# A two-layer decoder step on one core: gate logits with the weights stationary, an unsplit fp32 gather, last sums spread by 64-row tiles

## The chip, the cores and the metric

The kernel runs on one core of a Trainium2 chip. The time is device microseconds of that core; the time before is 1553.24 us, the median of three runs (1552.7 to 1557.6). In the profile, PE is TensorE's matmuls and PEld its weight loads, DVE is VectorE, ACT ScalarE, POOL GpSimd, SP SyncE, which issues nearly all loads. An fp32 matmul leaves two records in the trace; one whose operands are both of type fp32r leaves one.

## The reference, cut to what matters

One step of a two-layer model over T = 264 tokens (256 of a prompt, 8 of samples), D = 1024. Layer a has a gated DeltaNet mixer with 8 heads and a dense SwiGLU, layer b a pooling mixer and a top-2-of-8 mixture of experts; both attend to memory. The change touches three places of it.

```python
# layer_a: two logits for each head come from one projection
proj = u @ w_in
qkv, z, b_logit, a_logit, cq = jnp.split(proj, [o1, o2, o3, o4], axis=-1)
beta = jax.nn.sigmoid(b_logit)
g = -jnp.exp(a_log) * jax.nn.softplus(a_logit + dt_bias)
...
# layer_b: h + moe_swiglu(rmsnorm(h, norm2), ...)
logits = (x @ router_w).astype(jnp.float32)
top_v, top_i = lax.top_k(logits, TOP_K)
gates = jax.nn.softmax(top_v, axis=-1)
for e in range(N_EXPERTS):
    y = y + dispatch[..., e:e + 1] * swiglu(x, wi[e], wo[e])
...
y_prompt = rmsnorm(hp, final_norm)
```

## The kernel before

TensorE multiplies dense weights as split products: each 128x2048 tile of a weight comes by DMA into one of two draw slots, ACT copies its high part to fp32r (dense_high, L363), DVE subtracts to get the low part (dense_low, L369), and TensorE makes three fp32r products a pair (L1757). The tiles run in the order of the list DENSE. The draw slot is free once the low part exists; SP then issues the next load.

**Gate logits.** Before the input projection of layer a, 24 matmuls (L1821) take the normalised tokens u as the stationary operand, 128 tokens at a time, and the 16 columns of wba as the moving one; the token rows of logits land in bank 1. ACT copies them into gba (L661, L662) and runs exponent and logarithm for the gates; behind these in its queue stand the convolution history (L677), the evictions of the first projection tiles (L720) and the high part of the next weight. TensorE goes on with a_tile(0) and the rest (a_tile(t), 24 products each), once DVE has evicted the last memory values (mem_kv, L1029).

**Gather.** After the last b_out tile the router's logits are ranked on DVE; sel (rt_sub) goes to TensorE, which counts positions in each expert's list (bank 6). DVE makes a 0/1 matrix disp for each of three token tiles (L1589) and the normalised token rows xtok (token_rows, L1576). ACT and DVE split xtok into xth and xtl (L935, L1597); TensorE runs four unread matmuls on a ring chunk (L2290), then 48 passes of 96 columns that gather the first expert's tokens, feature-major, high into PP[3], low into PP[2] (L2297); ACT copies the one and DVE adds the other (L940, L1611). That is xs_ready for the first expert step.

**Experts.** A step serves 96 slots of one expert (C = SG x SL = 3 x 32). up(c) for 32 chunks makes 3 x 4 matmuls of 448 columns each, slots stationary, four at a time in column strips of 32 (L2316); down(j) for 14 chunks makes 12 of 512 columns (L2326) into banks 6 and 7, where slots 64 to 95 lie in bank 7 (z2) as two halves of the sum. The weights stream through a ring of 14.7 MB: 16 up chunks or 14 down chunks. SP issues a load as soon as TensorE has used the chunk that lay there (w_used; load_up L462, load_down L466). The rows of each step go to DRAM (slot_rows) by POOL's queue, and the next step's rows come from there and are turned in blocks of 32x32 by DVE (L1709). The number of steps is read from nsteps_i; eight run here.

**Last sums.** In the last step TensorE turns the matrix chosen (last_rows, L2351); POOL fetches each token's rows of the earlier steps (L590), DVE adds them (L1669). The last step's own rows go by matmul: rows_out puts the pieces of banks 6 and 7 together in yslot (L1675 to L1680), ACT and DVE split them (L959, L1717), TensorE spreads them to tokens by 12 matmuls (L2373), and DVE adds, normalises and hands on (last_part L1729, final L1735; ACT squares in L969).

Of the kernel before, what the change touches and what calls it, by code (L numbers as in the profile page):

```python
# [26 lines left out]
P = 128  # L27
D = 1024
# [41 lines left out]
LOADS = [3] * RDOWN + [2] * (RUP - RDOWN)  # L70
EARLIER = [2, 2, 2, 2, 3, 3, 2] + [0] * 9
# [42 lines left out]
def build(nc, ins, outs):  # L114
    ctx = ExitStack()
    with ctx:
# [9 lines left out]
        wba = sb("wba", KD * 16)  # L126
# [74 lines left out]
        assert 22336 + 2 * 12 * T == WREG  # L201
        cq = cut(gen, 0, XH * T).rearrange("p (m c) -> p m c", m=XH)
# [70 lines left out]
        disp = gat_("disp", 13312, 3 * C, F32R)  # L273
        xth = gat_("xth", 3072, 3 * D, F32R)
        xtl = gat_("xtl", 6656, 3 * D, F32R)
# [50 lines left out]
        picked, posb = cut(small, 760, 32), cut(small, 792, 32)  # L326

# [52 lines left out]

        def by_quarters(t, n):
            return xtok[0:n, t, :].rearrange("p (q k i) -> p k q i", q=4, k=KD)

        def turned_view(x, t, n):
            return x[0:n, t * D:(t + 1) * D].rearrange("p (k q i) -> p k q i", q=4, k=KD)

        def gathered(out):
            return out[:, :].rearrange("p (k n) -> p k n", n=P)[:, :, 0:C].rearrange("p k (s c) -> p s k c", s=SG)
# [134 lines left out]
        def _(pool):  # L523
# [38 lines left out]
            for x in (xth, xtl):  # L562
                pool.memset(x[:, 2 * D:3 * D].bitcast(F32), 0.0).then_inc(s("rest_zero"), 1)
# [32 lines left out]
        def _(a):  # L596
# [66 lines left out]
            a.wait_ge(s("gba_out"), 2)  # L663
# [250 lines left out]
            for t in range(KD - DSET):  # L914
                next_high(AT["b_out", t])
                if t == 4:
                    a.wait_ge(s("xt_mm"), 4)
                    a.wait_ge(s("zeroed"), 5)
                    token_square(2, 0, slice(0, 512))
                    a.activation(home[2][0:NS, 0:512], bank(5)[0:NS, :], ACT.Copy).then_inc(s("xt_out"), 1)  # L920
# [1550 lines left out]
```

## Time and profile before

| | us |
|---|---|
| median of three runs | 1553.24 |
| the profiled execution | 1551.51 |
| its span, first to last instruction | 1549.9 |
| PE busy | 1517.6 (98%) |
| DVE busy | 568.1 (37%) |
| ACT busy | 358.3 (23%) |
| mean granted TensorE clock | 0.990 of 2.4 GHz |
| chain: share of L2316 + L2326 | 37% + 19% |
| chain: share of L1757 | 24% |

The numbers are of one execution. A line of the chain gives the start, the length, the engine, the tile written, the line and how many records. In a timeline a bracket at the end is the time for which the engine was idle before, and what ended that. In the table by stretches, busy time for each of the five rows of engines is followed by the count of instructions, then come the granted clock as a share of full speed, the share of the DMA engines that is busy, and GB/s. A busy TensorE is not one at its peak: ends of matmuls are modelled.

### The profile page before, as it was taken

To read this page: it belongs to the slowest core of one execution; us is meant where nothing else is said; L and a number is where in the kernel's file an instruction comes from. 1 tells how busy PE (TensorE), PEld (TensorE's weight loads), DVE (VectorE), ACT (ScalarE), POOL (GpSimd) and SP (SyncE) were. 2 spreads that over 40 slices of the span, in tenths; PEclk is the share of its full clock that TensorE was granted. 3 is DMA by queue.
4 is the path that set the end of the run, shared out by engine and by line. 5 is a ranking of instruction groups with operands and counts; after the bars stand their busy time and mean duration, and the time that the engine had idled before them with its cause. 6 is when DMAs were issued, how large, how long until landed. Compare 5 with 4: busy or idle time off the path is not lost.

```text
span 1549.9 us, 32644 instructions
## 1 busy us (share of the span) xinstructions
PE 1517.6 (98%) x14378; PEld 883.2 (57%) x14378; DVE 568.1 (37%) x948; ACT 358.3 (23%) x587; POOL 60.4 (4%) x101
## 2 busy tenths in 40 slices
PE   8999999899999999999999999999999999999996
PEld 8989888899999999833233233232332332332332
DVE  6767878666665577510111101101101101111114
ACT  6466544444443453410000000000000000000001
POOL 0000031000000000020000000000000000000010
PEclk9999999999999999999999999999999999999998
DMA  7764358254554575799999999999999999999993
GB/s 266 286 234 175 110 190 261 72 204 170 185 190 150 196 301 198 277 404 416 419 401 419 419 400 420 418 400 420 401 419 419 400 419 419 400 420 418 419 416 122
DMA packets 78053, 490.97 MB, mean 317 GB/s; under 512 B 9305, under 2 KB 9561, under 8 KB 53217
## 3 DMA queue, kind: packets, MB, share of 16 engines
q1 hardware_dynamic: 70000, 460.71, 74.7%
q0 software_dynamic: 7920, 28.25, 5.6%
q8 instruction: 113, 1.85, 0.5%
q14 instruction: 20, 0.16, 0.0%
HBM read 465.00 MB, written 23.92 MB: 315 GB/s over the span
## 4 chain that ended last, share of the span: by engine, by line
PE 89%; DVE 5%; ACT 3%; DMA 2%; issue 1%; SPq 0%; DVEq 0%; ACTq 0%
PE PP L2316 37%; PE PP L1757 24%; PE PP L2326 19%; PE PP L2062 1%; PE PP L2072 1%; DVE dlo L369 1%; ACT dhi L363 1%; DMA ring<-in_mkv 1%; PE PP L1869 0%; PE PP L1853 0%; PE PP L2202 0%; PE PP L1845 0%; PE PP L2050 0%; PE PP L1831 0%; DMA ring<-in_a_out 0%
## 5 line engine op out<-in xcount | busy, mean ns | idle before, releaser
L2316 PE MATMUL PP<-ring,gen 128*32 128x448 f32 x6144 | 581.2, 541 | 1.0 <-DVE gen L1611 1.0
L2316 PEld LDWEIGHTS PP<-ring,gen 128*32 128x32 f32 x6144 | 185.0, 110 | 396.1 <-issue 394.9
L2326 PE MATMUL PP<-ring,gen 128*32 128x512 f32 x2688 | 289.8, 592 | 0.0
L1694 DVE TENSOR_TENSOR gen<-ubuf,PP 128x448 f32<-128x448 f32 x48 | 26.9, 616 | 519.1 <-PE PP L2316 519.1
L1757 PE MATMUL PP<-uh,dhi 128*128 128x264 f32 x736 | 214.4, 291 | 1.8 <-DVE dlo L369 1.1
L369 DVE TENSOR_TENSOR dlo<-ring,dhi 128x2048 fp32r<-128x2048 f32 (+2 forms) x85 | 175.5, 2064 | 98.0 <-ACT dhi L363 97.7
L1757 PE MATMUL PP<-ul,dhi 128*128 128x264 f32 x736 | 210.1, 285 | 0.0
L1757 PE MATMUL PP<-uh,dlo 128*128 128x264 f32 x736 | 209.8, 285 | 0.0
L952 ACT ACTIVATE ubuf<-PP 128x448 f32<-128x448 f32 x48 | 22.6, 545 | 782.6 <-PE PP L2316 782.6
L2326 PEld LDWEIGHTS PP<-ring,gen 128*32 128x32 f32 x2688 | 81.5, 110 | 205.7 <-issue 205.7
L363 ACT ACTIVATE dhi<-ring 128x2048 fp32r<-128x2048 f32 (+2 forms) x85 | 147.1, 1730 | 106.0 <-PE PP L1757 80.6
L1757 PEld LDWEIGHTS PP<-uh,dhi 128*128 128x128 f32 x736 | 140.0, 190 | 7.6 <-issue 5.4
L1757 PEld LDWEIGHTS PP<-ul,dhi 128*128 128x128 f32 x736 | 140.0, 190 | 0.2
L1757 PEld LDWEIGHTS PP<-uh,dlo 128*128 128x128 f32 x736 | 139.4, 189 | 0.0
L1675 DVE COPY gen<-PP 32x512 f32<-32x512 f32 x16 | 11.0, 686 | 231.7 <-PE PP L2326 231.5
L1757 PE MATMUL PP<-cath,dhi 128*128 128x264 f32 x192 | 56.3, 293 | 1.8 <-DVE dlo L369 1.8
L1757 PE MATMUL PP<-cath,dlo 128*128 128x264 f32 x192 | 55.2, 287 | 0.0
L1757 PE MATMUL PP<-catl,dhi 128*128 128x264 f32 x192 | 55.2, 287 | 0.0
L1757 PE MATMUL PP<-hidh,dhi 128*128 128x264 f32 x176 | 50.3, 286 | 0.6 <-DVE dlo L369 0.6
L1757 PE MATMUL PP<-hidh,dlo 128*128 128x264 f32 x176 | 50.0, 284 | 0.0
L1757 PE MATMUL PP<-hidl,dhi 128*128 128x264 f32 x176 | 49.8, 283 | 0.0
L1757 PEld LDWEIGHTS PP<-cath,dhi 128*128 128x128 f32 x192 | 36.7, 191 | 3.1 <-DVE dlo L369 2.4
(457 smaller groups left out, 1387.5 us busy)
## 6 DMA issues: line engine op xcount, KB each, us to landing
ring<-in_w_up SPq DMA_DIRECT2D x256, 896.0 KB, 22.6
ring<-in_w_down SPq DMA_DIRECT2D x112, 1024.0 KB, 23.1
ring<-in_wi SPq DMA_DIRECT2D x22, 1024.0 KB, 4.8
ring<-in_a_in SPq DMA_DIRECT2D x18, 1024.0 KB, 5.2
ring<-in_wo SPq DMA_DIRECT2D x16, 704.0 KB, 4.0
slot_rows<-ring POOLq DMA_DIRECT2D x25, 384.0 KB, 16.0
ring<-in_mkv SPq DMA_DIRECT2D x8, 1024.0 KB, 5.1
ring<-in_kc SPq DMA_DIRECT2D x8, 1024.0 KB, 9.3
```

The lines of the kernel that those rows point to most:

```text
L363: a.activation(halves(n)[0], x, ACT.Copy).then_inc(s("d_hi"), 1)
L369: v.tensor_tensor(low, draw[n % DRAW][:, 0:WIDTH[DENSE[n][0]]], high.bitcast(F32), ALU.subtract)\
L952: a.activation(esil[g], bank(g)[:, 0:FQ], ACT.Silu).then_inc(s("up_sil"), 1)
L1675: v.tensor_copy(yslot[2 * SL:C, 512 * h:512 * (h + 1)], z2[64 * h:64 * h + SL, :]).then_inc(s("y_part"), 1)
L1694: v.tensor_tensor(hslot[g], esil[g], bank(SG + g)[:, 0:FQ], ALU.mult).then_inc(s("up_h"), 1)
L1757: mm = pe.matmul(out, lhs[l], rhs[r], start=first and i == 0, stop=last and i == 2)
L2062: mm = pe.matmul(PP[c][:, head(x)], MLb[c][:, head(x)], Tb[c][:, head(x)], start=True, stop=True)
L2072: mm = pe.matmul(PP[c][:, head(x)], Xb[c][:, head(x)], Ub[c][:, head(x)], start=True, stop=True)
L2316: mm = pe.matmul(bank((c // KD % 2) * SG + g)[SL * q:SL * (q + 1), 0:FQ], xs[:, at_:at_ + SL], w[:, q * FQ:(q + 1) * FQ], start=(k == 0), ...
L2326: return pe.matmul(out[SL * quarter:SL * (quarter + 1), :], hT[:, at_:at_ + SL], w[:, k * D + h * 512:k * D + (h + 1) * 512], start=(j == ...
```

## The change

Three edits in one kernel. (1) Gate logits: wba is padded to 32 columns for each k and becomes the stationary operand, u the moving one; the eight k go to four strips of 32 columns, two each. ACT copies the 128x264 result, and after a_tile(0) three small matmuls with sel16 (a 0/1 matrix that DVE sums from ident) add the four strips and turn them to token rows (gate_columns). wba moves into the area of cq. (2) Gather: xtok and disp stay fp32 and unsplit; disp is stationary in groups of 32 slots, xtok moves in four quarters of 256 columns side by side; the result lies slot-major in banks 4, 6 and 7, and DVE turns it by block transposes straight from PSUM into xs. Of the four unread matmuls two go ahead of the wait for rt_sub. POOL zeroes xtok's third tile. (3) Last sums: banks 7 and 6 are copied whole, by DVE as soon as the last z2 product is done and by ACT at the end, and are spread as they stand: chosen holds each slot's row where it lies in those banks, TensorE turns six 128x128 tiles of it, and multiplies 64 rows by 32 columns at a time. Semaphore counts follow; sd_cols and sd_blk are merged.

```diff
+GATHER_BANK = [4, 6, 7]
...
+        wba = cut(gen, 0, KD * 32)
...
-        disp = gat_("disp", 13312, 3 * C, F32R)
-        xth = gat_("xth", 3072, 3 * D, F32R)
-        xtl = gat_("xtl", 6656, 3 * D, F32R)
+        disp = cut(gen, 13312, 3 * C)
...
-        yth, ytl = gat_("yth", 3072, D, F32R), gat_("ytl", 6656, D, F32R)
...
-        spread = gat_("spread", 8704, 384, F32R)
-        chosen = cut(gen, 9088, 3 * C)
+        spread = cut(gen, 8000, 3 * 2 * P)
+        yz = [cut(yslot, 0, 512), cut(yslot, 512, 512)]
+        chosen = cut(gen, 9088, 3 * 2 * P)
...
+        sel16 = cut(small, 824, 16)
...
-            for x in (xth, xtl):
-                pool.memset(x[:, 2 * D:3 * D].bitcast(F32), 0.0).then_inc(s("rest_zero"), 1)
+            pool.memset(xtok[:, 2, :], 0.0).then_inc(s("rest_zero"), 1)
...
             a.wait_ge(s("logits_mm"), 1)
+            a.activation(rt[:, 0:T], bank(1)[:, 0:T], ACT.Copy).then_inc(s("gba_out"), 1)
+            a.wait_ge(s("logits_mm"), 2)
...
-            a.wait_ge(s("rest_zero"), 2)
-            for t in range(3):
-                n = P if t < 2 else NS
+            for t in range(2):
                 a.wait_ge(s("xt_tok"), t + 1)
-                a.activation(turned_view(xth, t, n), by_quarters(t, n), ACT.Copy).then_inc(s("xt_hi"), 1)
-            for t in range(2):
                 a.activation(home[t], PP[t][:, :], ACT.Copy).then_inc(s("xt_out"), 1)
 
-            a.wait_ge(s("gat_mm"), 1)
-            a.activation(xs.rearrange("p (s k c) -> p s k c", s=SG, k=KD), gathered(PP[3]), ACT.Copy).then_inc(s("xt_out"), 1)
...
                     a.wait_ge(s("pos_mm"), 2)
-                    a.activation(spread[0:C, :], bank(0)[0:C, 0:384], ACT.Copy).then_inc(s("xt_hi"), 1)
+                    a.activation(spread, PP[0][:, 0:3 * 2 * P], ACT.Copy).then_inc(s("xt_hi"), 1)
                     a.activation(yroot[:, 0:1], epsc[:, 0:1], ACT.Sqrt)
-                    for g in range(2):
-                        a.wait_ge(s("y_part"), st * 2 + (g + 3))
-                        a.activation(yth[0:C, g * 512:(g + 1) * 512], yslot[0:C, g * 512:(g + 1) * 512], ACT.Copy)\
-                            .then_inc(s("xt_hi"), 1)
+                    a.wait_ge(s("w_used"), st * PERX + PERX)
+                    a.wait_ge(s("y_stored"), st * 16 + 16)
+                    a.activation(yz[0], bank(6), ACT.Copy).then_inc(s("xt_hi"), 1)
...
+            v.reduce_sum(sel16, ident.rearrange("p (g c) -> p c g", g=4)[:, 0:16, :], AX).then_inc(s("zeroed"), 1)
...
+            v.wait_ge(s("rest_zero"), 1)
             token_rows(2)
-            v.wait_ge(s("rest_zero"), 2)
-            for t in range(3):
-                n = P if t < 2 else NS
-                v.wait_ge(s("xt_hi"), t + 1)
-                v.tensor_tensor(turned_view(xtl, t, n), by_quarters(t, n), turned_view(xth, t, n).bitcast(F32), ALU.subtract).then_inc(s("xt_lo"), 1)
...
-            v.wait_ge(s("gat_mm"), 2)
-            v.wait_ge(s("xt_out"), 5)
-            xs4 = xs.rearrange("p (s k c) -> p s k c", s=SG, k=KD)
-            v.tensor_tensor(xs4, xs4, gathered(PP[2]), ALU.add).then_inc(s("xs_ready"), 1)
+            v.wait_ge(s("gat_mm"), 1)
+            for g in range(SG):
+                ins_ = v.transpose(xs[:, g * 2 * P:(g + 1) * 2 * P], bank(GATHER_BANK[g])[:, 0:2 * P])
+            ins_.then_inc(s("xs_ready"), 1)
...
-                    v.tensor_scalar(chosen[:, t * C:(t + 1) * C], iota[:, 0:C], row_late[:, t:t + 1], None, ALU.is_equal)\
-                        .then_inc(s("disp"), 1)
+                    for at_, n, slots in ((0, 2, iota[:, 0:2 * SL]), (P, 4, iota[:, 2 * SL:C])):
+                        v.tensor_scalar(chosen[:, 2 * t * P + at_:2 * t * P + at_ + P].rearrange("p (n c) -> p n c", n=n),
+                                        slots.unsqueeze(1).to_broadcast([P, n, P // n]), row_late[:, t:t + 1], None, ALU.is_equal)\
+                            .then_inc(s("disp"), 1)
...
-                v.wait_ge(s("w_used"), st * PERX + PERX)
                 v.wait_ge(s("y_stored"), st * 16 + 16)
-                rows_out(st, last)
                 if last:
-                    for g in range(2):
-                        v.wait_ge(s("xt_hi"), g + 5)
-                        v.tensor_tensor(ytl[0:C, g * 512:(g + 1) * 512], yslot[0:C, g * 512:(g + 1) * 512],
-                                        yth[0:C, g * 512:(g + 1) * 512].bitcast(F32), ALU.subtract).then_inc(s("xt_lo"), 1)
+                    v.wait_ge(s("z2_done"), 1)
+                    v.tensor_copy(yz[1], bank(7)).then_inc(s("xt_lo"), 1)
+                else:
+                    v.wait_ge(s("w_used"), st * PERX + PERX)
+                    rows_out(st)
...
-            for t in range(3):
-                n = P if t < 2 else NS
-                for k in range(KD):
-                    mm = pe.matmul(bank(1)[0:n, 16 * t:16 * t + 16], u[:, k, t * P:t * P + n], wb[:, k, :],
-                                   start=(k == 0), stop=(k == KD - 1))
+            for k in range(KD):
+                j = k % 4
+                mm = pe.matmul(bank(1)[32 * j:32 * j + 32, 0:T], wb[:, k, :], u[:, k, :], start=(k < 4), stop=(k >= 4))
             mm.then_inc(s("logits_mm"), 1)
+
+            def gate_columns():
+                pe.wait_ge(s("gba_out"), 1)
+                pe.wait_ge(s("zeroed"), 2)
+                for t in range(3):
+                    n = P if t < 2 else NS
+                    mm = pe.matmul(bank(1)[0:n, 16 * t:16 * t + 16], rt[:, t * P:t * P + n], sel16, start=True, stop=True)
+                mm.then_inc(s("logits_mm"), 1)
...
-            for t in range(5):
+            a_tile(0)
+            gate_columns()
+            for t in range(1, 5):
...
+            pe.wait_ge(chunk_loaded[0], 16 * EARLIER[0] + 16)
+
+            def unread(count):
+                for _ in range(count):
+                    pe.matmul(bank(7), up_of(0)[:, 0:P], up_of(0)[:, 0:512], start=True, stop=True)
+
+            unread(2)
...
-            pe.wait_ge(s("xt_out"), 2)
-            pe.wait_ge(chunk_loaded[0], 16 * EARLIER[0] + 16)
-            for _ in range(4):
-                pe.matmul(bank(5), up_of(0)[:, 0:P], up_of(0)[:, 0:512], start=True, stop=True)
-            pe.wait_ge(s("disp"), 3)
-            pe.wait_ge(s("rest_zero"), 2)
-            for x, done, out in ((xth, "xt_hi", PP[3]), (xtl, "xt_lo", PP[2])):
-                pe.wait_ge(s(done), 3)
-                for k in range(KD):
-                    for t in range(3):
-                        mm = pe.matmul(out[:, k * P:k * P + C], x[:, t * D + k * P:t * D + (k + 1) * P], disp[:, t * C:(t + 1) * C], start=(t == 0), stop=(t == 2))
-                mm.then_inc(s("gat_mm"), 1)
+            unread(2)
+            pe.wait_ge(s("rest_zero"), 1)
+            for t in range(3):
+                pe.wait_ge(s("disp"), t + 1)
+                pe.wait_ge(s("xt_tok"), t + 1)
+                for g in range(SG):
+                    for q in range(4):
+                        mm = pe.matmul(bank(GATHER_BANK[g])[SL * q:SL * (q + 1), 0:2 * P], disp[:, t * C + g * SL:t * C + (g + 1) * SL],
+                                       xtok[:, t, 2 * P * q:2 * P * (q + 1)], start=(t == 0), stop=(t == 2))
+            mm.then_inc(s("gat_mm"), 1)
             pe.wait_ge(s("xt_out"), 4)
-            pe.wait_ge(s("xt_tok"), 2)
...
-                def down(j):
+                def down(j, apart=False):
                     landed(st, j, 2)
                     w = down_of(j)
 
@@ -2329,7 +2321,9 @@
 
                     for h in range(2):
                         for k in range(2):
-                            product(z2, 2 * h + k, 2, k, h)
+                            mm = product(z2, 2 * h + k, 2, k, h)
+                    if apart:
+                        mm.then_inc(s("z2_done"), 1)
...
-                    pe.wait_ge(s("disp"), 6)
-                    pe.wait_ge(s("up_sil"), st * (2 * SG) + (SG + 1))
-                    for t in range(3):
-                        mm = pe.transpose(bank(0)[0:C, t * P:(t + 1) * P], chosen[:, t * C:(t + 1) * C], ident)
+                    pe.wait_ge(s("disp"), 9)
+                    pe.wait_ge(s("up_sil"), st * (2 * SG) + (SG + 2))
+                    for t in range(6):
+                        mm = pe.transpose(PP[0][:, t * P:(t + 1) * P], chosen[:, t * P:(t + 1) * P], ident)
                     mm.then_inc(s("pos_mm"), 1)
                 pe.wait_ge(s("y_out"), st + 1)
                 for j in range(NDOWN):
                     if j in (0, NDOWN // 2):
                         pe.wait_ge(s("h_turned"), st * 2 + (1 if j == 0 else 2))
-                    down(j)
+                    down(j, last and j == NDOWN - 1)
...
-            pe.wait_ge(s("xt_hi"), 4)
+            pe.wait_ge(s("xt_hi"), 1)
             for t in range(3):
-                n = P if t < 2 else NS
-                for g in range(2):
-                    for x, done, had in ((yth, "xt_hi", 5), (ytl, "xt_lo", 4)):
-                        if t == 0:
-                            pe.wait_ge(s(done), g + had)
-                        mm = pe.matmul(PP[t][0:n, g * 512:(g + 1) * 512], spread[0:C, t * P:t * P + n], x[0:C, g * 512:(g + 1) * 512],
-                                       start=(done == "xt_hi"), stop=(done == "xt_lo"))
+                n = SL if t < 2 else NS
+                for z, done, count in ((1, "xt_lo", 1), (0, "xt_hi", 2)):
+                    if t == 0:
+                        pe.wait_ge(s(done), count)
+                    for x in range(2):
+                        rows_ = slice(64 * x, 64 * x + 64)
+                        for q in range(4 if t < 2 else 1):
+                            at_ = (2 * t + z) * P + SL * q
+                            mm = pe.matmul(bank(2 * t + x)[SL * q:SL * q + n, :], spread[rows_, at_:at_ + n], yz[z][rows_, :],
+                                           start=(z == 1), stop=(z == 0))
```

## Rows read from the trace of the kernel before

**Rows 1.** The page: GB/s moved by the DMA, in 40 equal slices of the span.
```profile
GB/s 266 286 234 175 110 190 261 72 204 170 185 190 150 196 301 198 277 404 416 419 401 419 419 400 420 418 400 420 401 419 419 400 419 419 400 420 418 419 416 122
```

**Rows 2.** The chain that ended last: start us, us, engine, tile, line, count.
```profile
60.88 4.12 PE PP L1821 x48
...
362.77 116.30 PE PP L1757 x960
...
663.23 74.83 PE PP L2316 x768
...
774.12 72.16 PE PP L2316 x768
...
1496.00 36.23 PE PP L2326 x336
```

**Rows 3.** Line L466 (down loads): one issue each near 731 and 1486 us, and landing.
```profile
L466 SPq DMA_DIRECT2D ring<-in_w_down x1: 333/333/333, 731.5 to 731.5; - x1
...
DMA to landing us min/median/max: 16.2/16.2/16.2
...
L466 SPq DMA_DIRECT2D ring<-in_w_down x1: 328/328/328, 1486.6 to 1486.6; - x1
...
DMA to landing us min/median/max: 31.1/31.1/31.1
```

**Rows 4.** Busy time by engine, then granted clock (PEclk), DMA share, GB/s, by stretch.
```profile
65.00:66.00 1.00, 1.00 (x5) 1.00 (x6) 0.57 (x3) 0.95 (x3) 0.00 (x0) 0.50 1.08 328
...
652.00:654.00 2.00, 2.00 (x4) 0.88 (x3) 1.97 (x6) 0.75 (x2) 0.00 (x0) 0.50 1.02 427
```

**Rows 5.** The chain again: matmuls in column strips (L1853, L1896) and row strips (L2036).
```profile
90.23 1.86 PE PP L1853 x32
...
122.33 0.48 PE PP L1896 x8
...
239.27 1.14 PE PP L2036 x8
```

**Rows 6.** Timelines of DVE, then of ACT, 60 to 80 us: start, us, what, [idle before].
```profile
61.07 0.87 DVE L1029 TENSOR_SCALAR gen<-PP,gen 128x256 f32<-128x256 f32 x2
...
74.53 2.29 DVE L369 TENSOR_TENSOR dlo<-ring,dhi 128x2048 fp32r<-128x2048 f32 x1 [4.93 <-ACT dhi L363]
...
65.03 0.20 ACT L661 ACTIVATE small<-PP 128x32 f32<-128x32 f32 x1 [2.15 <-PE PP L1821]
...
72.50 1.91 ACT L363 ACTIVATE dhi<-ring 128x2048 fp32r<-128x2048 f32 x1
...
78.05 0.39 ACT L720 ACTIVATE gen<-PP 128x264 f32<-128x264 f32 x1 [2.53 <-PE PP L1757]
```

**Rows 7.** The chain from 650 to 664 us: the third token row tile, then the gather.
```profile
653.86 1.27 DVE gen L1576
...
656.35 5.84 PE PP L2297 x48
...
662.22 0.96 DVE gen L1611
```

**Rows 8.** Timelines of 640 to 670 us, and of DVE from 735 us.
```profile
647.57 0.60 ACT L911 ACTIVATE ubuf<-PP 128x512 f32<-128x512 f32 x1 [8.61 <-PE PP L2224]
...
650.59 5.38 PE L2290 MATMUL PP<-ring 128*128 128x512 f32 x8
...
741.54 1.05 DVE L1709 STREAM_TRANSPOSE gen<-gen 128x256 f32<-128x256 f32 x3
```

**Rows 9.** Timeline of the last 18 us, DVE's rows.
```profile
1532.35 1.40 DVE L1675 COPY gen<-PP 32x512 f32<-32x512 f32 x2 [9.62 <-PE PP L2326]
...
1539.05 1.28 DVE L1729 SCALAR_TENSOR_TENSOR gen<-PP,gen 128x1024 f32<-128x1024 f32 x1 [1.08 <-PE PP L2373]
...
1540.76 1.28 DVE L1729 SCALAR_TENSOR_TENSOR gen<-PP,gen 128x1024 f32<-128x1024 f32 x1 [0.42 <-PE PP L2373]
...
1546.34 1.27 DVE L1735 SCALAR_TENSOR_TENSOR gen<-gen 8x1024 f32<-8x1024 f32 x1
```

More of the change, by code:

```diff
@@ L125, in build @@
         gains = sb("gains", GN)
-        wba = sb("wba", KD * 16)
         router = sb("router", KD * E)
@@ L379, in cache_of @@
             return cut(ring, ARENA + x * 2048, 2048)
[L381 to L388, printed above, removed]
         def new_state(v, r):
@@ L662, in _ @@
             a.activation(gba[0:NS, 2, :], bank(1)[0:NS, 32:48], ACT.Copy).then_inc(s("gba_out"), 1)
-            a.wait_ge(s("gba_out"), 2)
+            a.wait_ge(s("gba_out"), 3)
             a.activation(gb, gba[:, :, 0:8], ACT.Exp, scale=-1.0).then_inc(s("gate_exp"), 1)
@@ L917, in _ @@
                     a.wait_ge(s("xt_mm"), 4)
-                    a.wait_ge(s("zeroed"), 5)
+                    a.wait_ge(s("zeroed"), 6)
                     token_square(2, 0, slice(0, 512))
@@ L1086, in _ @@
             next_low(7)
-            v.wait_ge(s("gba_out"), 2)
+            v.wait_ge(s("gba_out"), 3)
             dt_b = gains[:, GDT:GDT + H].unsqueeze(1).to_broadcast([P, 3, H])
@@ L1111, in _ @@
             v.wait_ge(s("conv_rows"), NS)
-            v.wait_ge(s("zeroed"), 2)
+            v.wait_ge(s("zeroed"), 3)
             def prompt_max(l, t):
@@ L1180, in _ @@
                     l2_scale(4, 8)
-            v.wait_ge(s("logits_mm"), 2)
+            v.wait_ge(s("logits_mm"), 3)
             link(v.tensor_copy(cG, bank(5)[:, 0:16]))
@@ L1229, in sample_columns @@
                 v.tensor_copy(padded(kpad), by_group(kq[:, :, 0]))
-                v.tensor_tensor(kqd, kq[:, :, 0], kq[:, :, 1], ALU.mult).then_inc(s("sd_cols"), 1)
+                v.tensor_tensor(kqd, kq[:, :, 0], kq[:, :, 1], ALU.mult).then_inc(s("sd_in"), 1)
             def level_mask(lv, c):
@@ L1321, in block @@
                 v.tensor_tensor(ublk[r % 2].rearrange("p (n c) -> p n c", c=P), urow.unsqueeze(1).to_broadcast([P, 4, P]),
-                                own16[:, 4 * r:4 * r + 4].unsqueeze(2).to_broadcast([P, 4, P]), ALU.mult).then_inc(s("sd_blk"), 1)
+                                own16[:, 4 * r:4 * r + 4].unsqueeze(2).to_broadcast([P, 4, P]), ALU.mult).then_inc(s("sd_in"), 1)
             for lv in range(1, NLVL):
@@ L1461, in _ @@
             ins_.then_inc(s("zeroed"), 1)
-            v.wait_ge(s("zeroed"), 4)
+            v.wait_ge(s("zeroed"), 5)
             def pooled(n):
@@ L1554, in _ @@
                     v.memset(yslot, 0.0).then_inc(s("y_out"), 1)
-            v.wait_ge(s("logits_mm"), 3)
+            v.wait_ge(s("logits_mm"), 4)
             link(v.tensor_copy(rout, bank(4)[:, 0:3 * E]))
@@ L1670, in collect, with rows_out @@
                                        in1=(home, y1)[j][t][0:n, :], op0=ALU.mult, op1=ALU.add).then_inc(s("y_sum"), 1)
-            def rows_out(st, last):
+            def rows_out(st):
                 z1, z2 = bank(6), bank(7)
@@ L1680, in rows_out @@
                     ins_ = v.tensor_tensor(half, half, z2[64 * h + SL:64 * (h + 1), :], ALU.add)
-                    if last:
-                        ins_.then_inc(s("y_part"), 1)
-                    elif h:
+                    if h:
                         ins_.then_inc(s("y_out"), 1)
@@ L1828, in scores @@
                 if l == 0 and t == 0:
-                    pe.wait_ge(s("gba_out"), 2)
+                    pe.wait_ge(s("gba_out"), 3)
                 for x in range(XH):
@@ L2017, in _ @@
             pe.wait_ge(s("dl_mt"), 4)
-            pe.wait_ge(s("sd_cols"), 1)
+            pe.wait_ge(s("sd_in"), 1)
             pe.wait_ge(s("state_loaded"), 64)
@@ L2029, in outer @@
             def outer(r):
-                pe.wait_ge(s("sd_blk"), r + 1)
+                pe.wait_ge(s("sd_in"), r + 2)
                 if r == 0:
@@ L2427 @@
         "grow2": rows(f["b_norm2"]),
-        "wba": w_in[:, split:split + 16].reshape(KD, P, 16).transpose(1, 0, 2).reshape(P, -1),
+        "wba": np.pad(w_in[:, split:split + 16].reshape(KD, P, 16), ((0, 0), (0, 0), (0, 16))).transpose(1, 0, 2).reshape(P, -1),
         "router": f["b_router"][0].reshape(KD, P, E).transpose(1, 0, 2).reshape(P, -1),
```

1 line of the change is left out of this document (removed).

## The prediction

> **What bounds the kernel now.** I read the page's slices first, then the chain that ended last, then the landing times of the expert weights, and at last the timelines and the granted clock around the three places that the change touches. In the slices the reader is to see two halves: up to about 660 us the DMA comes and goes, from there on it moves about 419 GB/s in nearly every slice but the last [rows 1]. The chain gives that second half to TensorE: each of eight expert steps is 72.16 us of up products (74.83 in the first) and some 36.2 of down products, with nothing between [rows 2]. So TensorE is the bound by the chain. The landing times say how near DMA is to being it too. The twelfth down load of the first step (index 11) was issued at 731.5 and landed 16.2 later, at 747.7 [rows 3]; TensorE needed it at 663.23 + 74.83 + 11 x 2.588 = 766.5 (36.23 / 14 = 2.588 a down tile) [rows 2], a lead of 18.8 us. The tenth (index 9) of the last step was issued at 1486.6 and landed 31.1 later, at 1517.7 [rows 3]; its use is at 1496.00 + 9 x 2.588 = 1519.3 [rows 2]. The lead has melted to 1.6 us. A load is issued when its ring slot comes free, and the time to land has grown from 16 to 31 us: the queue always holds work, and delivers a little more slowly than TensorE eats. This reading decides most here.
>
> **Part 1, gate logits.** Now 24 matmuls with u stationary, 16 columns each, take 4.12 us (L1821) [rows 2], and TensorE comes out of them at its 1.2 GHz level: 0.50 is granted from 65 to 66 us [rows 4]. The change runs 8 matmuls of 264 columns, their weights 32 columns wide, in four column strips: two groups of four. Four strips with 288 columns took 0.48 [rows 5], so two groups of 264 take 0.88. ACT copies the sums out while it has nothing else to do, and three small matmuls after a_tile(0) turn them to token rows: six records at 4.12 / 48 = 0.09, 0.5 us. A tile of the input projection is 24 records, 116.30 / 40 = 2.91 [rows 2]. New order on TensorE: logits until 61.8; a_tile(0) must wait for DVE's last memory value, made at 61.94 [rows 6], and the added reduce_sum stands ahead of it in DVE's queue for some 0.2, so 62.1; gates end at 62.1 + 2.9 + 0.5 = 65.5; three more tiles end at 74.3, where ACT saw the fourth tile end at 78.05 before [rows 6]. For TensorE that is 3.7 us. Late next is ACT's queue: the gate copies and their chain (two table loads, eight history copies) stand ahead of the evictions and of the next high half. The gate copy ran at 65.03 and will run at about 65.6, so the chain behind it moves back by 0.6. The high half of a_in 2 started at 72.50, because it stood behind an eviction that waited for TensorE; now it starts at about 71.0, right behind the gates and two evictions that find their tiles done, and the low half ends 4.3 us later (72.50 to 74.53 + 2.29 now) at 75.3 [rows 6]. TensorE waits 1 us there. Net **-2.8 us**. Bounds: -4.4 (all of 4.12 and about 1.2 of slow start, less 0.88, if ACT holds nothing back) and -1.5 (only what the high half moves by). From there to 645 us the chain runs from TensorE through ACT and DVE back to TensorE, all of it released by TensorE, so the shift is carried on; the expert loads wait for the last b_out tile and start as much sooner.
>
> **Part 2, the gather.** Removed: high halves on ACT (L935), low halves on DVE (L1597), 48 passes of 96 columns (5.84 us, L2297), ACT's copy (L940), DVE's addition (0.96, L1611) [rows 7]. Added: 36 matmuls of 256 columns in four strips, three groups per token tile, and three block transposes from PSUM. DVE's chain sets the order: the third token row tile runs from 653.86 to 655.13 [rows 7]. The four unread matmuls ran from 650.59 for 5.38 us [rows 8], mostly at the low level (0.50 granted from 652 to 654 [rows 4]), after an idle stretch in which TensorE waited for rt_sub. Two of them now run in that stretch. At 2.4 GHz one takes 0.86 (512 columns, by 72.16 / 96 = 0.75 for four strips of 448 side by side [rows 2], which stream as long as one), so two are done when rt_sub comes, the other two by 652.5, and the clock has less reason to fall. With DVE as it is until 655.13, the last token tile's three groups start at 655.2. A group costs 1.86 / 4 = 0.465 by L1853 [rows 5], or 256/448 of 0.75 = 0.43 by the up products [rows 2]: 1.35 in all, until 656.6. Three transposes took 1.05 from SBUF (L1709) [rows 8]; from PSUM between that and 1.3, at 656.6 + 1.2 = 657.8 experts start, not at 663.23: -5.4. With a high clock the first up phase also loses its slow start, 74.83 - 72.16 = 2.67 [rows 2]. The move offers **8.0 us**; with the clock as low as before (groups and unread matmuls twice as long) about 2. ACT's copies of the residual (home) and the step count come earlier too, as their queues lose the halves, and hold nobody.
>
> **How much of the 8.0 is kept.** A faster start does not empty the DMA queue, which holds 16 to 31 us of work throughout. The loads' start does not move with the gather, so their landings don't. A TensorE that starts 8 us sooner only runs into them: the lead falls from 18.8 by some 2.4 us a step now; from 10.8 it is gone before the last steps, and these wait for weights. The down products end no sooner than 1517.7 + 5 x 2.588 = 1530.6 [rows 3] against 1496.00 + 36.23 = 1532.23 [rows 2]. Kept: **-1.6 us**. Six 128x128 transposes in place of three 128x96 ones (some 0.5 us more in the last step) vanish in the same wait, as do the six wider DVE writes in last_rows. Ends of this term: 0 (in another execution the landings come that much later) and -7.5 (they come earlier, and only the transposes cost).
>
> **Part 3, the last sums.** Now DVE puts four pieces together from 1532.35 on, ACT and DVE split them, TensorE multiplies 12 times, DVE adds tile 0 at 1539.05 and tile 1 at 1540.76, and its last instruction starts at 1546.34 [rows 9]. After: bank 7 is complete a third into the last down tile, so DVE's copy of it hides under the rest; ACT copies bank 6 (0.60, as its square of 128x512 from PSUM [rows 8]) while TensorE multiplies the other half. Then eight matmuls of 64 rows x 32 columns x 512 per half and tile. No row shows this shape. Four row strips of 32 at 512 columns took 1.14 (L2036) [rows 5], four column strips would take 0.86. If both directions combine, eight cost 0.9 to 1.1; if one does, 1.7 to 2.1; if none does, 6.9. I take 1.0, since each kind is seen to overlap. From the end of the down products (1532.23 in the old times) tile 0 is ready at 1534.3, tile 1 at 1536.3. Behind tile 1 DVE and ACT run as now: 1540.76 - 1536.3, **-4.4 us**. At 2.0 per eight, tile 1 comes at 1540.3 and the gain is 0.5.
>
> The Trainium skill has a rule that speaks against the strips of all three parts: TensorEngine Tiling (Array Packing), section Key Properties, says that a change of tiling mode drains the engine. The page gives no price; by it the sum would rise by one drain for each of some eight added changes. The trace shows no such gap where the last step goes from strips to whole-array transposes and back.
>
> **The sum.** -2.8 - 1.6 - 4.4 = -8.8 us. The profiled execution took 1551.51 (span 1549.9 and 1.6 around it), so 1542.7. The median of the runs shown, 1553.24, is 1.7 above it; I carry that over: **1544.5**.
>
> **The rivals.** (a) The landings have room that the issue rule hides, and the gather keeps 7.5: -2.8 - 7.5 - 4.4 = -14.7, 1538.5. For it: TensorE has no wait for a weight in this profile. Against: the time to land doubles over the steps. The Trainium skill's page DMA: Bandwidth & Descriptors, section Where 436 GB/s comes from, puts the ceiling at 435 GB/s; at that rate weights would come in time, which gives (a), but the slices hold about 419. (b) Strips of 64 rows and of 32 columns don't combine: -2.8 - 1.6 - 0.5 = -4.9, 1548.3. (c) Most is eaten: ACT's queue leaves -1.5 of part 1, the landings are no earlier than the old need, and the last sums run at 1.2 GHz: -2.5, 1550.7. For it: a lead of 1.6 us is smaller than the 4.9 between the three runs. (d) Slower: 64-row matmuls overlap with nothing. Place: the last sums; tile 1 comes at 4 x 6.9 = 27.6 behind the down products, not at 8.5: +19.1 - 4.4 = +14.7, 1568. It decides from 3.2 us per eight, where 4 x 3.2 = 8.5 + 4.4. Against it: each kind of strip overlaps.
>
> **Chances.** Forecast 0.54, (a) 0.13, (b) 0.18, (c) 0.11, (d) 0.04. The range goes from (a) past (b): 1538.5 to 1549, and leaves out (c) and (d). About 0.3% (4.7 us) is what a measurement of this kernel can tell from no change, so 1548.6 parts faster from same: the forecast, (a) and two thirds of (b) lie below, 0.79; the rest of (b) and (c) are same, 0.17; (d) is slower, 0.04.
>
> **What would show it.** Gates: tile 4 of a_in starts 2.8 us sooner, after about 1 us of waiting for DVE's low half. Gather: the first up product comes 5.4 us sooner behind the last b_out tile, at 2.4 GHz. Experts: the first steps last 108.4 us, the last ones more, with TensorE waiting for ring<-in_w_up and in_w_down; if no such wait appears, (a) holds. Last sums: about 1 us per eight matmuls, and 13.3 us from the last down product to the end of the span in place of 17.7. A time above 1549 would mean that strips don't combine or the leads were gone already.

## The result, and the profile after

The changed kernel takes 1544.44 us (median, 1543.83 to 1547.69) where the kernel before takes 1554.99 in the same comparison: ratio 0.9933, 95% interval 0.9922 to 0.9944. The forecast was 1544.5. The profiled execution took 1544.28; its span, first to last instruction, is 1542.5, 7.4 us less than before.

The slices of the page (GB/s, in 40 slices of the span), to compare with [rows 1]. The second half moves what it moved before:

```profile
GB/s 265 294 243 165 110 191 263 82 194 167 190 181 162 182 301 197 273 398 418 419 399 420 419 402 419 412 408 420 403 418 420 401 419 419 402 419 419 418 416 186
```

Part 1 in the chain of waits, 61 to 79 us (start, length, engine, tile, line, records), to compare with [rows 2, 6]:

```profile
61.32 0.80 DVE gen L1014 x2
...
62.16 3.20 PE PP L1738 x24
65.36 0.50 PE PP L1809 x6
...
71.19 1.81 ACT dhi L363
...
73.12 2.30 DVE dlo L369
75.42 0.04 issue
75.47 3.19 PE PP L1738 x24
```

The gates and their turning (L1809) are over at 65.86, and a_in tile 4 starts at 75.47 behind DVE's low half, as the prediction had it (75.3). In the kernel before, that tile's first matmul starts at 77.85 and the next work behind it at 80.78; here these are 75.47 and 78.50. So at 80 us the shift is 2.3 us, not 2.8.

Part 2 in the same view, to compare with [rows 7, 8]:

```profile
646.68 1.80 PE PP L2271 x4
...
649.77 1.80 PE PP L2271 x4
651.57 1.44 PE PP L2289 x24
653.00 0.10 issue
653.10 2.83 PE PP L2289 x48
655.93 0.02 issue
655.95 1.12 DVE gen L1592 x3
657.08 0.04 issue
657.12 12.22 PE PP L2308 x125
```

L2271 are the unread matmuls, L2289 the gather (36 matmuls of two records, 4.27 us), L1592 the block transposes. Experts start 12.7 us behind the end of the last b_out tile (640.01 + 4.39 = 644.40), before 17.8. The granted clock is 1.00 from 640 to 672 us, where [rows 4] had 0.50.

The end of the experts and the last sums, to compare with [rows 2, 9], first in the chain and then DVE's first addition in the timeline:

```profile
1480.84 33.12 DMA ring<-in_w_down
1513.96 0.04 issue
1514.01 15.66 PE PP L2318 x144
1529.66 3.69 PE PP L2370 x64
1533.35 0.02 issue
1533.38 1.28 DVE gen L1710
...
1538.96 1.27 DVE gen L1716
```

```profile
1531.66 1.28 DVE L1710 SCALAR_TENSOR_TENSOR gen<-PP,gen 128x1024 f32<-128x1024 f32 x1 [2.88 <-PE PP L2370]
```

And the waits of TensorE's weight loads (PEld) for landings between 652 and 1535 us (total, times, longest), of which the kernel before had none:

```profile
PEld PP L2308 <- DMA ring<-in_w_up: 8.9, 24, 1.4
PEld PP L2318 <- DMA ring<-in_w_down: 5.6, 10, 1.3
```

Landings now hold up the end of the expert phase: what releases the last 144 records of down products (L2318) is a load that was under way for 33.12 us, queue included. TensorE itself did not stand still that long: its longest wait is 1.4 us, and the totals of 8.9 and 5.6 us are idle time of its weight loads, part of which lies under running matmuls. From the start of the last b_out tile to the end of the down products it is 889.65 us, before 891.23. From there to the end of the span, last sums included (L2370), it is 12.84, before 17.67. So the span's 7.4 us are 1.0 up to the last b_out tile (its start moves from 641.00 to 640.01), 1.6 in the gather and the experts, 4.8 at the end.

### The profile page after: what moved, and what is told of

It reads as the page before. It is cut to its first block, busy times and chain, and to the rows that moved or that the text cites. A ratio compares the mean times of both kernels' runs of the same rounds, so it can differ in the third digit from the quotient of the medians.

```text
span 1542.5 us, 32756 instructions
## 1 busy us (share of the span) xinstructions
PE 1511.4 (98%) x14439; PEld 1013.8 (66%) x14439; DVE 561.0 (36%) x944; ACT 354.5 (23%) x583; POOL 59.5 (4%) x100
## 4 chain that ended last, share of the span: by engine, by line
PE 79%; DMA 6%; DVE 6%; SPq 4%; ACT 3%; issue 1%; DVEq 0%; ACTq 0%
PE PP L2308 33%; PE PP L1738 22%; PE PP L2318 15%; DMA ring<-in_w_down 2%; SPq L453 2%; DVE dlo L369 2%; SPq L457 2%; DMA ring<-in_w_up 2%; ACT dhi L363 2%; PE PP L2051 1%; PE PP L2061 1%; DMA ring<-in_mkv 1%; PE PP L1856 1%; PE PP L1840 0%; PE PP L2191 0%
## 5 line engine op out<-in xcount | busy, mean ns | idle before, releaser
L2308 PEld LDWEIGHTS PP<-ring,gen 128*32 128x32 f32 x6144 | 294.6, 110 | 287.1 <-issue 259.9
L2318 PE MATMUL PP<-ring,gen 128*32 128x512 f32 x2688 | 293.2, 592 | 1.8 <-DMA ring<-in_w_down 1.8
L2318 PEld LDWEIGHTS PP<-ring,gen 128*32 128x32 f32 x2688 | 112.2, 110 | 179.0 <-issue 159.9
```

The source lines that it names most:

```text
L2308: mm = pe.matmul(bank((c // KD % 2) * SG + g)[SL * q:SL * (q + 1), 0:FQ], xs[:, at_:at_ + SL], w[:, q * FQ:(q + 1) * FQ], start=(k == 0), ...
L2318: return pe.matmul(out[SL * quarter:SL * (quarter + 1), :], hT[:, at_:at_ + SL], w[:, k * D + h * 512:k * D + (h + 1) * 512], start=(j == ...
```

## The experiments

**Each part alone.** The kernel before with the hunks of one of the three edits, and semaphore counts to match (in the last sums alone, for instance, `(1, "xt_lo", 4), (0, "xt_hi", 5)`, as the old gather has counted before). 

> The kernel before with part 1 alone (gate logits with weights stationary, turned after tile 0). Theory: the shift of 2.3 us at 80 us is partly given back between 320 and 361 us, where weight landings stand in the chain of waits, so about 1.0 us is left at the end of the last b_out tile and at the end: ratio 0.9993, 0.9990 to 0.9998. Rival (everything behind is released by TensorE, the shift arrives whole): -2.3 to -2.8 us, ratio 0.9982 to 0.9985. The last b_out tile ends at 644.1 by the theory, at 642.4 by the rival (645.1 before).

> The kernel before with part 2 alone (gather from unsplit fp32 tiles, four unread matmuls in two places). Theory: experts start about 5.1 us earlier and the first one runs 2.7 us faster at the full clock, but from then on weight landings bind: downs end 1.6 us earlier (1530.6 against 1532.2), ratio 0.9990 (0.9986 to 0.9994). Rival (the 1.6 us left in the changed kernel are an interaction with the other two parts, alone it gives the 8.0 us): ratio 0.9949. TensorE waits for in_w_up and in_w_down are near 0 by the rival, 10 us or more by the theory.

> The kernel before with part 3 alone (last sums from both banks copied whole, in 64-row tiles). Theory: it stands behind everything and nothing gives it back: from the end of the last downs to the end of the span 12.8 us instead of 17.7, -4.8 us, ratio 0.9969 (0.9965 to 0.9973). Rival (part of the 4.8 us comes with the landing-bound end of the downs in the changed kernel): -3 us or less, ratio 0.998. The three parts alone should add up to -7.4 us, the gain of the whole.

Measured: ratios 0.9992 (0.9982 to 1.0002), 0.9995 (0.9986 to 1.0004) and 0.9973 (0.9964 to 0.9982). Of the three only the last is clear of no change; for the others the traces must tell. Part 3 alone: 13.17 us from the down products to the end, -4.5. Part 2 alone: experts start 5.1 us sooner behind the last b_out tile, TensorE's weight loads then wait 27.6 us for in_w_up and 11.4 for in_w_down, and 0.5 us is left (890.71 against 891.23); the rival's 8.0 is out. Part 1 alone: the last b_out tile starts at 640.27, 0.7 us sooner. That is nearer to the theory's 1.0 than to 2.3, but one pair of traces doesn't settle it (this start varies by 1.4 us between traces with the same gates, see below), and the interval of the time reaches both. Whether the parts add up was to be seen beside the whole, on another chip:

> The changed kernel once more, timed beside the next three on one chip. Theory (the parts add up): the parts alone gave ratios 0.9992, 0.9995 and 0.9973, product 0.9960, so 0.9945 to 0.9960 here. Rival (the parts help each other): 0.9933 as in the first comparison or lower.

Measured 0.9941 (0.9928 to 0.9953), 1545.65 against 1554.9, between the theory's range and the rival. Each part alone is uncertain by 0.0009 or 0.0010, their product 0.9960 by some 0.0016, so the intervals meet and neither reading is excluded; the pauses told of below may be a reason why the ratio of the whole differs from chip to chip.

**A later start of the experts.**

```
-            unread(2)
+            unread(6)
             pe.wait_ge(s("rest_zero"), 1)
```

> The changed kernel with six unread matmuls in place of the second two, ahead of the gather: its start moves by four times 0.90 us = 3.6 us. Theory (weight landings bind the experts): the end does not move, 1544.4 us, at most +0.5; TensorE's waits for in_w_up and in_w_down shrink by about 3.6 us. Rival (TensorE binds, the gather's gain went elsewhere): +3.6 us, 1548.0 us.

Measured 1544.91 us (1544.07 to 1547.67), ratio 0.9956 (0.9944 to 0.9968). The changed kernel wasn't timed on this chip, so the times don't decide: its medians elsewhere are 1544.44 and 1545.65, but its ratios 0.9933 and 0.9941 would make the late start 2 to 4 us slower, and the kernel before alone has medians from 1551.8 to 1555.0 on the chips used here. The traces do decide. Experts start at 660.08, 3.1 us later behind the last b_out tile than in the changed kernel, and the down products end 890.80 us behind that tile's start. The two profiles of the changed kernel have 889.65 and 890.08, both with a pause of TensorE told of below; the half in_wi kernel at the end of this section, which from 365 us on is the changed kernel but for which token goes to which expert, and has no such pause in the first steps, has 890.07. So of 3.1 us later, 0.7 (against the last) to 1.15 arrive, more than the theory's 0.5 and far less than the rival's all. The waits of TensorE's weight loads:

```profile
PEld PP L2318 <- DMA ring<-in_w_down: 7.0, 13, 1.9
PEld PP L2308 <- DMA ring<-in_w_up: 5.4, 13, 1.0
```

They shrank by 2.1 us. Most of a shift of the start is lost, in either direction: landings bind.

**Earlier loads.**

```
-            for c in range(RUP):
+            for c in [0, 1, 2, 3, 15, 9, 8, 10, 11, 4, 5, 6, 7, 12, 13, 14]:
...
+                if c == 15:
+                    sp.wait_ge(s("outputs_stored"), 32)
+                if c in (9, 8):
+                    sp.wait_ge(s("d_lo"), TURN[AT["b_out", 6 if c == 9 else 7]] + 1)
+                if c == 10:
+                    sp.wait_ge(s("bout_mm"), KD - 1)
                 if c == 4:
                     sp.wait_ge(s("bout_mm"), KD)
-                    sp.wait_ge(s("outputs_stored"), 32)
                     sp.wait_ge(s("rows_zeroed"), 16 * (NST + 1))
                 load_up(0, c)
```

> The changed kernel with SyncE's first 16 expert loads in another order: after chunks 0 to 3 come chunk 15 (its place in the ring is free once the pool states are stored), 9 and 8 (free once the low parts of the last two b_out tiles are taken), 10 and 11 (free after the seventh b_out tile), then 4 to 7 and 12 to 14 after the eighth as now. The DMA queue then works through the 5 us around 640 in which it now stands still. Theory: TensorE becomes the bound again, downs end at 1523.3 to 1524.8 instead of 1529.7, time 1538.0 to 1539.6 (-4.9 to -6.4 us against the changed kernel, ratio 0.989 to 0.990 to the kernel before). Rival: no change, 1544.4 us.

> Early loads as above and six unread matmuls as above, together. Theory: now TensorE is the bound, so the later start of 3.6 us that costs nothing in the changed kernel costs nearly all of itself: +2.2 to +3.6 us against the early loads alone, about 1541.6 us. Rival: the same time as early loads alone.

> The kernel before with SyncE's early loads alone. Theory: before, TensorE was the bound of the experts without a wait for weights in the trace, so earlier weights give nothing: ratio 1.000 (0.9995 to 1.0005). Rival (the DMA queue was the bound before too, or the landings disturb the b_out loads): -2 us or more, or +1 us or more.

Measured: 1537.75 us, ratio 0.9905 (0.9891 to 0.9920); with the late start 1543.14, 0.9943 (0.9931 to 0.9955); on the kernel before 1.000 (0.9992 to 1.0009). All three go the theory's way; the first is 0.3 us below its range, and the late start costs 5.4 us where at most 3.6 were expected. How busy the DMA engines were from 630 to 650 us (tenths, slices of 0.5 us), first in the changed kernel, then with early loads, and the latter's chain at the end:

```profile
DMA  9999999999989999998600000000004859998999
```

```profile
DMA  9979999999999999999999999999998999997999
```

```profile
1479.87 7.14 PE PP L2313 x76
1487.01 0.81 PE PP L2350 x6
1487.81 36.19 PE PP L2323 x336
1524.00 3.69 PE PP L2375 x64
```

The gap of 5 us at 640 is filled. Every phase of ups is 72.16 us (72.4 in the first step) and every phase of downs 36.05 (36.2 in the last), with no DMA in the chain, and from the start of the last b_out tile to the end of the downs it is 883.93, 7.3 us less than before: nearly the whole 8.0 that part 2 offers. With the late start it is 887.06: the same 3.1 us of later start, of which 0.7 to 1.15 arrived above, now arrive whole. The medians differ by 5.4; the other 2.3 lie in executions that have no trace, and some 1.0 of them outside the span (time less span is 2.3 to 2.8 us in five of the six, 1.6 to 1.8 with early loads alone). Early loads give the lowest time of all versions here; they were timed beside the kernel before, not beside the changed kernel, but the intervals of the two ratios (up to 0.9920, from 0.9922) don't meet.

**Lighter weights.** Three quarters of the columns of each expert weight tile behind the first 16 are loaded, every matmul is kept, and the outputs are other ones.

```
+                half = UCH if isinstance(e, int) and e == 0 else UCH * 3 // 4
-                sp.dma_start(up_of(c), ...)
+                sp.dma_start(up_of(c)[:, 0:half], ...[:, 0:half])
```

> The kernel before with only three quarters of the columns of each expert weight tile loaded (the first 16 up tiles are loaded whole; the rest of the columns keep what stood there, so the y output is another one; every matmul stays). Theory: TensorE bound the experts before, each step 108.2 us, so a quarter less to load gives nothing: ratio 0.9995 to 1.0005. Rival (landings bound it too): -2 us or more.

> The changed kernel with the same three quarters of the weights (y is another output). Theory: TensorE binds again and the whole 8.0 us of the gather come through, downs end 883.3 to 884.0 us after the last b_out tile has begun instead of 889.7, time 1538.0 to 1539.5 like early loads, -5 to -6.4 us against the changed kernel beside it. Rival (the gather's gain was not lost to landings): the same time as the changed kernel.

Measured: 1.0004 (0.9995 to 1.0014) and 0.9915 (0.9902 to 0.9927), 1541.85 us; beside them the changed kernel had 1545.65. Before, weights cost nothing; changed, they do: -3.8 us, on one chip, where 5 to 6.4 were expected. The traces show the missing part. In both light kernels TensorE loses 1.2 to 1.8 us at each of two places, with nothing that the profile names as holding it (called a pause here). The second of these in the chain, e9 and then e10:

```profile
1498.18 8.70 PE PP L2328 x74
1506.88 0.19 issue
1507.07 28.57 PE PP L2328 x262
```

```profile
1490.22 8.70 PE PP L2320 x74
1498.92 0.23 issue
1499.15 28.55 PE PP L2320 x262
```

The last down phase is 37.5 us in both, against 36.2 [rows 2]; the first up phase is 1.7 us longer too. Together that is 3.0 us of the 3.3 by which e9 is longer than the kernel before (894.52 from the start of the last b_out tile to the downs' end, before 891.23), and of the same size in e10 (886.92 where early loads have 883.93). Between the two light kernels lie 894.52 - 886.92 = 7.6 us, the 8.0 of the gather less its longer transposes.

**No unread matmuls**, on early loads.

```
-            unread(2)
             pe.wait_ge(s("rt_sub"), 1)
...
-            unread(2)
             pe.wait_ge(s("rest_zero"), 1)
```

> The kernel with early loads (TensorE-bound, 1537.8 us) without the four unread matmuls. Theory of the clock: TensorE idles 1.9 us before and 2 us after the place matmuls, the granted clock falls to 0.50 near 652, the gather and the start of the first expert run slow: first expert 110.9 instead of 108.4 us, experts start up to 4.3 us later, together +2.7 to +6 us. Rival (the unread matmuls do nothing): 0.

Measured 1544.28, ratio 0.9933 (0.9919 to 0.9947), on another chip than the early loads (1537.75, 0.9905). Stretches of 2 us (busy time of PE, PEld, DVE, ACT, POOL; then granted clock, DMA share, GB/s) and the gather in the chain:

```profile
650.00:652.00 2.00, 0.33 (x5) 0.23 (x8) 1.90 (x8) 1.02 (x1) 0.00 (x0) 0.55 1.00 416
652.00:654.00 2.00, 2.00 (x24) 1.04 (x20) 2.00 (x3) 0.77 (x1) 0.00 (x0) 0.50 1.01 419
654.00:656.00 2.00, 2.00 (x25) 0.98 (x21) 1.22 (x9) 1.54 (x2) 0.00 (x0) 0.50 1.05 427
```

```profile
651.75 6.72 PE PP L2292 x72
```

TensorE is busy for 0.33 of the 2 us from 650 to 652; it is granted 0.50, its 1.2 GHz level, from 652 to 656, and the gather takes 6.72 us in place of 4.27. Experts start 2.3 us later behind the last b_out tile (659.66 - 640.26 against 657.17 - 640.07). The clock was back at 1.00 before they began, so the forecast 110.9 us for the first step, which lays the extra time on a low clock, has the wrong reason although 110.5 was measured. Of 5.6 us between the traces (889.53 against 883.93), 2.3 are the clock's; the other 3.3 are the two pauses just described, which this trace has (its first up phase 74.4, its last down phase 37.5 us) and the one with early loads has not. The 6.5 us between the medians can't be divided so, the less as they come from two chips.

**Where part 1 is given back.** Of the 2.3 us at 80 us the first pair of traces had 1.0 left at the last b_out tile. More traces say more: the times of three events over the 13 traces with whole dense weights (five with the old gates, eight with the new; means in us):

| | old gates | new gates | shift |
|---|---|---|---|
| POOL issues the store of S | 317.02 | 314.55 | -2.5 |
| chain reaches TensorE's split products again, around 361 | 362.97 | 361.39 | -1.6 |
| last b_out tile starts | 641.44 (641.00 to 642.42) | 640.00 (637.85 to 640.95) | -1.4 |

These means are of few traces. From one trace to the next the first and the last of the three vary by 1.4 to 3.1 us, so the last shift is known to about 0.9 only. Measured inside each trace, the way from the first to the last is 1.0 us longer with the new gates (324.42 and 325.45 in the mean, the difference uncertain by about 0.8), so part of the shift is indeed given back. Between the first two ScalarE takes the first in_wi tile. Its timeline in the changed kernel, and then the chain of the kernel before:

```profile
339.21 1.49 ACT L363 ACTIVATE dhi<-ring 128x1536 fp32r<-128x1536 f32 x1 [2.17 <-PE PP L1738]
...
344.27 1.92 ACT L363 ACTIVATE dhi<-ring 128x2048 fp32r<-128x2048 f32 x1 [2.85 <-DMA ring<-in_wi]
```

```profile
337.97 7.44 PE PP L1757 x61
...
345.49 1.93 ACT dhi L363
```

From one high half to the next it is 4.38 us in all five traces with the old gates, released by TensorE, and 4.76 to 5.08 in all eight with the new, released by the landing. With half a tile to load, the landing should drop out:

```
+                width = WIDTH[kind] // 2 if kind == "wi" and i < 2 else WIDTH[kind]
-                sp.dma_start(draw[n % DRAW][:, 0:WIDTH[kind]], ins[kind][i])...
+                sp.dma_start(draw[n % DRAW][:, 0:width], ins[kind][i][:, 0:width])...
```

> The changed kernel with only half the columns of the first two in_wi weight tiles loaded (the rest keeps what stood there, so y and the routing differ; only the stretch to 365 us is read). In the changed kernel ScalarE begins the first of these tiles 5.06 us after the last in_a_out tile, released by the landing (issued 338.14, 6.11 us); before it was 4.38 us, released by TensorE. Theory (the landing gives back 0.7 us of the gates' shift here): the landing drops out of the chain of waits and the distance is 4.38 us again. Rival (the landing only seems to be the releaser; the order of the engines sets it): 5.0 us or more.

```profile
339.89 1.49 ACT L363 ACTIVATE dhi<-ring 128x1536 fp32r<-128x1536 f32 x1 [2.17 <-PE PP L1739]
...
344.27 1.92 ACT L363 ACTIVATE dhi<-ring 128x2048 fp32r<-128x2048 f32 x1 [2.17 <-PE PP L1739]
```

4.38 again: the landing gives back 0.4 to 0.7 us here. It does not show at 361 us in this trace, where the chain reaches the split products at 361.54 as in the first profile of the changed kernel: the tile before, at 339.89, was itself 0.7 later. The load takes longer in the changed kernel, and one thing is under way in its 7 us that isn't in the kernel before's (DMA queue: packets, MB, share; then the loads issued in the window, count, size, time to land; the second fence is of before):

```profile
q8 instruction: 1, 0.02, 0.8%
...
ring<-in_wi SPq DMA_DIRECT2D x2, 1024.0 KB, 6.1
```

```profile
ring<-in_wi SPq DMA_DIRECT2D x2, 1024.0 KB, 4.8
```

All eight traces with the new gates have that instruction fetch beside the load and 5.8 to 6.1 us; all five with the old have none, and 4.7 to 4.8. With half the bytes and the fetch it is 4.6. That the fetch makes the load slower is not shown: it was not tried by itself.

## Why the prediction came out right

**Part 1 was over-sized, twice.** The order on TensorE, a wait for the low half (0.7 us, 1 forecast) and its end (75.3, measured 75.42) hold. At 80 us the shift is 2.3 us, not 2.8, and three small readings make up the difference: tile 4 starts at 75.47; in the kernel before it started at 77.85, not at 78.05, which is when ACT saw the tile ahead of it end; and its first matmul takes 0.1 us longer behind the wait. The second wrong step is "all of it released by TensorE, so the shift is carried on". The chain of the kernel before itself has two stretches in which a DMA transfer is what is waited for:

```profile
316.59 3.92 DMA out_S<-gen
...
322.66 5.98 DMA ring<-in_a_out
```

With the new gates a landing of in_wi stands there too (338.14, 6.11 us in the changed kernel). Of 2.3 to 2.5 us the means keep 1.4, the two traces compared first 1.0. The start of the expert loads moved with the last b_out tile, as said.

**Part 2 and what is kept of it held.** Experts start 5.1 us sooner against 5.4; the transposes take 1.12 (1.2); the clock is full; then the lead is gone before the last steps and TensorE waits for in_w_up and in_w_down. Two readings were off without harm. The gather was to wait for DVE's third token row tile; it does not: TensorE multiplies from 651.57 to 655.93 nearly without a gap (4.27 us, 0.47 a group), and so ends 0.3 us later than forecast. And the down load issued at 731.5 [rows 3] is the eleventh of its step, not the twelfth: its use was at 763.9, so the first lead is 16.2 us, not 18.8, and melts by 2.1 us a step, not 2.4. From 8.2 us after the earlier start it is gone before the last steps all the same; the bound that gives the 1.6 us rests on the last step's load, which was read rightly. Kept are 1.6 us in the pair of traces, as forecast, 0.5 in part 2 alone and 1.2 in the second trace of the changed kernel (890.08). The experiments turned the reading of the landing times [rows 3] into a test: most of a later start is free, and earlier loads give 5.7 us (889.65 to 883.93), while earlier or lighter loads do nothing to the kernel before. Rival (a), landings with room, would have shown no wait. The Trainium skill's page DMA: Bandwidth & Descriptors, section Where 436 GB/s comes from, names 435 GB/s as the ceiling; the full slices of the changed kernel hold 398 to 420, and the highest with early loads, where the DMA engines are busy from 630 us on, is 420 too, so the measurement decides against using its figure here.

**Part 3 held and was a little better.** Both directions of strips combine: DVE adds tile 0 at 1531.66 and tile 1 at 1533.38, 16 matmuls of 64 rows apart, so 0.86 us per eight where 1.0 was taken. Tile 1 comes 3.7 us behind the down products (4.1 forecast, 8.5 before). Rivals (b) and (d) fall with it; of (c), the clock of the last sums and the landings came out better, and only part 1 arrived smaller than even its -1.5. The Trainium skill, TensorEngine Tiling (Array Packing), section Key Properties, says that a change of tiling mode drains the engine. The chain shows no idle piece where the engine changes over, neither from whole-array matmuls to the gather's strips (651.57) nor from the down products' strips to those of 64 rows (1529.66); a price inside the matmuls' own times, whose ends are modelled, is not excluded.

**The sum** was -8.8 us on the profiled execution and is -7.2 (-7.4 on its span): of the span's difference part 1 took 1.8 less, part 3 gave 0.4 more. That the median still met 1544.5 is luck in part: the offset of 1.7 us carried from profile to median was that of the kernel before, and the changed kernel's is 0.2. (The stated terms add up to 1544.4.) Against the kernel before in the same comparison, 1554.99, the gain of the medians is 10.5 us, and 9.3 in the second comparison, both more than the forecast 8.7 and than the 7.4 that the traces account for. The kernel before has executions from 1549.9 to 1558.1, the changed one from 1543.8 to 1548.5. The pauses offer a reason: a kernel that TensorE binds pays 3.0 us for them (e9), one bound by landings hides them (the first up phase of the changed kernel has one, 74.0 us for 72.4, and the total is 889.65, no more than the 890.07 without one). It is not shown for the unchanged kernel before, whose profile has none, so this stays open.

## What to carry to other kernels

Ahead of a stream that is nearly bound by DMA, time won on TensorE is kept only down to the lead of the landings: compare, for the first and the last step, when a load lands and when it is used, and if the lead melts, first look for idle DMA time before the stream and for ring places that are free sooner than the program's order asks. Count the loads when you pair one with its use: a slip of one tile was 2.6 us here. A shift of a few us that must travel through hundreds of us need not be carried whole: look in the chain of the kernel before for landings on the way. Judge such a shift over several traces: one pair said 1.0, the means 1.4. And compare times only within one chip: the medians of the same kernel differ by 3 us between chips here.

## What was not expected of the hardware

An instruction fetch of 0.02 MB lies beside the first in_wi load in every kernel with the new gates, and that load lands 1.1 to 1.3 us later than with the old. TensorE paused without a releaser for 1.7 to 2.0 us in the first up phase (at 669 to 677 us) and for 1.2 to 1.3 in the last down phase (at about 1499 to 1507), both near POOL's indirect transfers, in the light kernels and the one without unread matmuls, all run on one chip; both profiles of the changed kernel have the first of them; the eight traces from three other chips (parts alone, late start, the first three with early loads, half in_wi) have none in the first up phase. They cost some 3 us where TensorE is the bound. What releases them the profile doesn't name. Without the four unread matmuls the granted clock was 0.50 to 0.55 from 650 to 656 us, and back at 1.00 from 658 on, while before, with them at the later place, it was 0.50 at 652 to 654 and again from 662 to 668.
